# The opening of a two-layer transformer kernel, in quarters of the contraction

## The chip, the cores and the metric
The kernel runs on one core of a Trainium2 chip, as one program. The metric is the device time of one execution in microseconds (us). Engines: TensorE (PE, matmul; PEld its weight loads), VectorE (DVE), ScalarE (ACT), GpSimd (POOL), SyncE (SP, here only the issuer of DMAs). Each runs its own instruction list in order and waits on semaphores.

## The reference
Three layers on 256 tokens of width 1024, float32: one with sparse (top-k) attention and a gated convolution, one with pooling and latent attention, one with three attention branches. The change touches the start of the first:

```python
def first_block(x, c, ada_w, ada_b, ...):
    cond = jax.nn.silu(c)
    for l in range(DEPTH):
        mod = (cond @ ada_w[l] + ada_b[l])[:, None, :]
        sh_m, sc_m, g_m, sh_f, sc_f, g_f = jnp.split(mod, 6, axis=-1)
        h = x * (1.0 + sc_m) + sh_m
        if l % 2 == 0:
            e = l // 2
            y = even_mixer(h, ev_w_in[e], ev_conv_w[e], ev_w_out[e])
        ...
        x = layer_norm(DN_ALPHA * x + (1.0 + g_m) * y, ln_mix_g[l], ln_mix_b[l])
        ...
def even_mixer(h, w_in, conv_w, w_out):
    z = h @ w_in
    q, k, v, qi, ki, wi, bg, cg, xb = _split(z, EVEN_SIZES)
    ya = dsa_attention(q..., k..., v..., qi..., ki, wi)
    yb = bg * causal_dwconv(cg * xb, conv_w)
    return jnp.concatenate([ya, yb], axis=-1) @ w_out
```

In `dsa_attention` the index queries `qi`, index keys `ki` and weights `wi` give a score for each pair of tokens, of which the 64 highest are kept for each query; then softmax attention with 8 heads over q, k, v.

## The kernel before
**Units and precision.** Weights are cut into units of 256 columns (UC), 8 contraction blocks (kt) of 128 rows each, 1 MB. SP loads unit g into `raw[g % 2]` (`load_unit`), ScalarE rounds it into a high part `unit_hi` (`hi_unit`, L839), GpSimd subtracts to get the low part `unit_lo` (`lo_unit`, L727). The activations h are split likewise (`hh`, `hl`, from the whole `hf`). A product is high x high, high x low and low x high, summed in bank 4 + g % 2. Order of units: two of index queries (`G_QI`, g = 0, 1), `G_KI` (g = 2, index keys and weights, 192 columns), six of q, k, v (`G_QKV[DSA]`, g = 3 to 8; QKV 0 to 5 below), the convolution, the output.

**Waits in the loop of units.** SP loads unit g once the low part of unit g - 2 is made (`lo_up`). ScalarE converts unit g once unit g - 2 has filled its bank, for `unit_hi[g % 2]` is then free. TensorE starts on the high part and waits for the low one behind the first block of 128 columns.

**Modulation.** `cond @ ada_w` for the first layer's shift and scale (blocks 0, 1 and 2, 3 of 512 columns) is needed before h exists. Shift: VectorE sums `ada_w` row blocks times cond into 128 partial rows (`modulation_half`: half a is 4 contraction blocks x 512 columns, 1 MB), TensorE sums the partitions in one-column matmuls (`mod_columns`). Scale: TensorE multiplies directly (`mod_half`, cond as a one-column weight), ScalarE copies the row, and one-row matmuls turn it into columns. All 16 columns stand, then h is made for all of the contraction by VectorE and ScalarE (`h_columns`, `h_high`). The other halves (numbers 4 and up) are summed by VectorE between other work; their loads stand in SP's list beside those of certain units (`early`).

**Around it.** The small vectors are staged by POOL's DMAs and transposed on TensorE (`stage`), x is transposed in 16 steps (`transpose_rows`). After KI and QKV 0 come the index scores: heads 0 to 3, QKV 1, heads 4 to 7 (L1663). ScalarE applies relu, VectorE weights and adds them head by head (L2284, L2286), which frees the banks that the next heads write; ahead of that VectorE's list has the halves 4 to 7. Then VectorE takes the top 64, while TensorE does QKV 2 to 5.

Of the kernel before, what the change touches and what calls it, by code (L numbers as in the profile page):

```python
# [18 lines left out]
ALU = mybir.AluOpType  # L19
# [89 lines left out]
def build(nc, W, consts, out):  # L109
# [101 lines left out]
    turn(("modc", 0, 0), 6)  # L211
# [9 lines left out]
    ht_turns(0)  # L221
    for h in range(HEADS):
        turn(("idx", h), h % 4)
# [42 lines left out]
    with ctx:  # L266
# [123 lines left out]
        def down_home(d):  # L390

            if d in SPARE:
# [11 lines left out]
        mod_in = [sem(f"mod_in{i}") for i in range(2)]  # L404
# [27 lines left out]
                   FOX: (o_h[1], o_l[1]), MOBA: (o_h[2], o_l[2]), "stick": (o_h[0], o_l[0])}  # L432

# [154 lines left out]
        def _(sp_):  # L588
# [23 lines left out]
            def load_mod(e):  # L612

                if e >= 2:
                    sp_.wait_ge(mod_done, e - 1)
                s = e % 2
                sp_.dma_start(ada[2 + s].rearrange("p (t n) -> p t n", t=KD // 2), half_of(0, MOD_PE[e // 2], s)
                              ).then_inc(mod_in[s], 16)
# [209 lines left out]
        def _(act):  # L828
# [19 lines left out]
            def h_high(n, columns, scale, shift):  # L848

                evacuated(act, columns)  # L850
                if n == 0:

                    def whole(q):
                        o = full(act, ("ht", n, q))
                        for kt in (2 * q, 2 * q + 1):
                            ins = nc.scalar.activation(hf[:, kt, :], o[:, S * (kt % 2):S * (kt % 2 + 1)], ACT.Identity,
                                                       scale=scale[:, kt:kt + 1], bias=shift[:, kt:kt + 1])
                        ins.then_inc(free(("ht", n, q)), 1)

                    def high(q):  # L860
                        evacuated(act, ("ht", n, q))
                        k = slice(2 * q, 2 * q + 2)
                        nc.scalar.activation(hh[:, k, :], hf[:, k, :], ACT.Copy).then_inc(h_hi, 1)

                    whole(1)
                    high(0)
                    high(1)
                    whole(3)
                    high(2)
                    high(3)  # L870
                    return
# [155 lines left out]
            for i, j in enumerate(MOD_PE):  # L1027
                if i == 1:
                    hi_unit(0)
                act.wait_ge(mod_done, 2 * i + 2)  # L1030
                nc.scalar.activation(accg[0:1, AC * j:AC * (j + 1)], bank[4 + i][0:1, :], ACT.Copy).then_inc(mod_row, 1)
            h_high(0, ("modc", 0, 0), modT[:, 0, 8:16], modT[:, 0, 0:8])
            hi_unit(1)

# [222 lines left out]
        def _(pe):  # L1257
# [197 lines left out]
            def mod_columns(layer, parts, first=True, js=range(16)):  # L1455
# [3 lines left out]
                for i, part in enumerate(parts):  # L1459
                    for j in js:  # L1460
                        block = 6 * part + j // 4
                        k = P
                        if (layer, part) == (0, 0) and block in MOD_PE:
                            k = 1
                            pe.wait_ge(mod_row, MOD_PE.index(block) + 1)
                        elif j % 4 == 0:
                            summed(pe, layer, block)
# [3 lines left out]
                if j == 15:  # L1471
                    done(mm, name)

            def mod_half(e):

                i, s = e // 2, e % 2
                pe.wait_ge(mod_in[s], 16 * (i + 1))
# [1035 lines left out]
```

## Time and profile before

| | us |
|---|---|
| median of 3 runs (1187.02 to 1191.23) | 1189.29 |
| the profiled execution | 1187.67 |
| its span | 1185.9 |
| PE busy | 1127.9 (95%) |
| DVE busy | 538.6 (45%) |
| ACT busy | 590.7 (50%) |
| POOL busy | 831.8 (70%) |

The span is measured by the profiler from the first instruction to the last; the execution's own time has 1.8 us around it. Busy times overlap. Idle time of an engine is of interest where another one waits for it.

### The profile page before, as it was taken

To read this page: it belongs to the slowest core of one execution; us is meant where nothing else is said; L and a number is where in the kernel's file an instruction comes from. 1 tells how busy PE (TensorE), PEld (TensorE's weight loads), DVE (VectorE), ACT (ScalarE), POOL (GpSimd) and SP (SyncE) were. 2 spreads that over 40 slices of the span, in tenths; PEclk is the share of its full clock that TensorE was granted. 3 is DMA by queue.
4 is the path that set the end of the run, shared out by engine and by line. 5 is a ranking of instruction groups with operands and counts; after the bars stand their busy time and mean duration, and the time that the engine had idled before them with its cause. 6 is when DMAs were issued, how large, how long until landed. Compare 5 with 4: busy or idle time off the path is not lost.

```text
span 1185.9 us, 21675 instructions
## 1 busy us (share of the span) xinstructions
PE 1127.9 (95%) x8119; PEld 1033.5 (87%) x8119; DVE 538.6 (45%) x1120; ACT 590.7 (50%) x894; POOL 831.8 (70%) x297
## 2 busy tenths in 40 slices
PE   6899898999999988999999989999999999999997
PEld 2799788999998987989999969999999988999996
DVE  4668677965657684594323350433111333111112
ACT  0445425545453554545545434555776544455444
POOL 3567467988876634798788737566656776988885
PEclk9899998999999999999999999999999999999999
DMA  9987587999987354597666415434444544766652
GB/s 341 323 270 199 201 276 242 342 330 320 320 276 248 114 143 147 176 288 240 183 188 181 138 36 177 139 112 142 143 143 143 185 153 127 211 186 187 192 178 88
DMA packets 253485, 238.03 MB, mean 201 GB/s; under 512 B 18076, under 2 KB 216529, under 8 KB 253425
## 3 DMA queue, kind: packets, MB, share of 16 engines
q1 hardware_dynamic: 235104, 198.70, 54.4%
q10 hardware_dynamic: 17712, 38.28, 9.0%
q8 instruction: 41, 0.67, 0.2%
q0 software_dynamic: 608, 0.22, 0.1%
q14 instruction: 20, 0.16, 0.0%
HBM read 236.12 MB, written 1.05 MB: 200 GB/s over the span
## 4 chain that ended last, share of the span: by engine, by line
PE 68%; DMA 7%; ACT 7%; DVE 7%; POOL 6%; issue 3%; SPq 0%; ACTq 0%; DVEq 0%; POOLq 0%
PE bank L1270 16%; PE bank L1271 16%; PE bank L1272 16%; POOL unit_lo L727 5%; ACT unit_hi L839 3%; DMA raw<-in_ev_w_in 3%; PE bank L1304 2%; PE bank L1295 2%; DMA raw<-in_ffn_w_up 2%; PE bank L1408 2%; PE bank L1296 2%; DMA ada<-in_ada_w 2%; PE bank L1331 1%; DVE x L2029 1%; PE bank L1324 1%
## 5 line engine op out<-in xcount | busy, mean ns | idle before, releaser
L727 POOL TENSOR_TENSOR unit_lo<-raw,unit_hi 128x2048 fp32r<-128x2048 f32 (+4 forms) x88 | 348.1, 3960 | 231.5 <-ACT unit_hi L839 230.6
L1270 PE MATMUL bank<-h_hi,unit_hi 128*128 128x256 f32 x1152 | 327.8, 285 | 2.9 <-POOL unit_lo L779 2.9
L1271 PE MATMUL bank<-h_lo,unit_hi 128*128 128x256 f32 x1152 | 326.6, 284 | 0.0
L1272 PE MATMUL bank<-h_hi,unit_lo 128*128 128x256 f32 x1152 | 326.6, 283 | 0.0
L779 POOL TENSOR_TENSOR unit_lo<-raw,unit_hi 128x2048 fp32r<-128x2048 f32 (+1 forms) x70 | 257.2, 3674 | 70.1 <-ACT unit_hi L986 65.2
L1270 PEld LDWEIGHTS bank<-h_hi,unit_hi 128*128 128x128 f32 x1152 | 221.5, 192 | 8.3 <-issue 5.5
L1271 PEld LDWEIGHTS bank<-h_lo,unit_hi 128*128 128x128 f32 x1152 | 221.5, 192 | 2.5
L1272 PEld LDWEIGHTS bank<-h_hi,unit_lo 128*128 128x128 f32 x1152 | 221.4, 192 | 0.0
L839 ACT ACTIVATE unit_hi<-raw 128x2048 fp32r<-128x2048 f32 (+4 forms) x98 | 163.1, 1666 | 103.4 <-DMA raw<-in_ffn_w_up 28.6
L782 POOL TENSOR_TENSOR down<-raw_down,down 128x1024 fp32r<-128x1024 f32 x70 | 176.5, 2522 | 0.0
L2160 DVE SCALAR_TENSOR_TENSOR work<-bank,cols,work 128x254 f32<-128x254 f32 (+1 forms) x176 | 72.6, 474 | 130.2 <-ACT work L973 130.2
L1270 PE MATMUL bank<-down,y_hi 128*128 128x512 f32 x296 | 116.5, 394 | 1.8 <-issue 0.9
L1271 PE MATMUL bank<-down,y_hi 128*128 128x512 f32 x296 | 116.0, 392 | 0.0
L1272 PE MATMUL bank<-down,y_lo 128*128 128x512 f32 x296 | 115.2, 389 | 0.0
L986 ACT ACTIVATE unit_hi<-raw 128x2048 fp32r<-128x2048 f32 (+1 forms) x60 | 90.8, 1514 | 5.1 <-DMA raw<-in_ffn_w_up 4.2
L971 ACT ACTIVATE work<-bank,cols 128x256 f32<-128x256 f32 x44 | 20.9, 474 | 118.2 <-PE bank L1272 105.2
L2189 DVE TENSOR_TENSOR bank<-bank,work 128x256 f32<-128x256 f32 x32 | 13.8, 433 | 135.3 <-ACT work L976 135.3
L1295 PE MATMUL bank<-h_hi,unit_hi 128*128 128x256 f32 x272 | 70.0, 294 | 2.5 <-DVE h_full L2313 2.5
L1012 ACT ACTIVATE down<-raw_down 128x1024 fp32r<-128x1024 f32 x60 | 63.3, 1056 | 14.5 <-PE bank L1272 14.4
L1296 PE MATMUL bank<-h_lo,unit_hi 128*128 128x256 f32 x272 | 68.5, 288 | 0.0
L1270 PEld LDWEIGHTS bank<-down,y_hi 128*128 128x128 f32 x296 | 55.8, 189 | 12.3 <-issue 1.9
L1272 PEld LDWEIGHTS bank<-down,y_lo 128*128 128x128 f32 x296 | 55.6, 188 | 12.1
(361 smaller groups left out, 2180.3 us busy)
## 6 DMA issues: line engine op xcount, KB each, us to landing
raw<-in_ffn_w_up SPq DMA_DIRECT2D x88, 512.0 KB, 5.2
raw<-in_w_in SPq DMA_DIRECT2D x60, 512.0 KB, 4.5
raw_down<-in_ffn_w_down SPq DMA_DIRECT2D x44, 512.0 KB, 5.5
ada<-in_ada_w ACTq DMA_DIRECT2D x16, 1024.0 KB, 6.9
raw<-in_w_up SPq DMA_DIRECT2D x64, 256.0 KB, 3.0
raw_down<-in_w_down SPq DMA_DIRECT2D x32, 512.0 KB, 3.5
raw<-in_ev_w_in SPq DMA_DIRECT2D x28, 512.0 KB, 5.2
att<-in_ada_w ACTq DMA_DIRECT2D x14, 1024.0 KB, 7.3
```

What stands on the lines that cost most here:

```text
L727: nc.gpsimd.tensor_tensor(ul[g % 2][:, w], raw[g % 2][:, w], uh[g % 2][:, w].bitcast(F32), ALU.subtract).then_inc(lo_up, 1)
L779: nc.gpsimd.tensor_tensor(ul[s][:, 0:w], raw[s][:, 0:w], uh[s][:, 0:w].bitcast(F32), ALU.subtract).then_inc(lo_up, 1)
L782: nc.gpsimd.tensor_tensor(down[:, 1 - k, 1, :], rawd[1 - k][:, :], down[:, 1 - k, 0, :].bitcast(F32), ALU.subtract).then_inc(lo_dn, 1)
L839: nc.scalar.activation(uh[s][:, w], raw[s][:, w], ACT.Copy).then_inc(hi_up, 1)
L986: nc.scalar.activation(uh[s][:, 0:w], raw[s][:, 0:w], ACT.Copy).then_inc(hi_up, 1)
L1012: nc.scalar.activation(down[:, 1 - k, 0, :], rawd[1 - k][:, :], ACT.Copy).then_inc(hi_dn, 1)
L1270: nc.tensor.matmul(o, sh, mh, start=first, stop=False)
L1271: nc.tensor.matmul(o, sh, ml, start=False, stop=False)
L1272: return nc.tensor.matmul(o, sl, mh, start=False, stop=last)
L1295: nc.tensor.matmul(o[:, 0:S], uh[s][:, a], mh[:, kt, :], start=kt == 0, stop=False)
L1296: nc.tensor.matmul(o[:, 0:S], uh[s][:, a], ml[:, kt, :], start=False, stop=False)
L2160: return V.scalar_tensor_tensor(t[:, back:S], bank[4 + s][:, S * j:S * (j + 1) - back], w, t[:, back:S], ALU.mult, ALU.add)
```

## The change
The shift and scale of the first layer are made in four quarters of 256 columns, which are two contraction blocks (kt) of h each. For a quarter, SP loads 2 MB in four DMAs (`load_first`), VectorE sums the shift in 8 steps of 256 columns (`first_sum`), TensorE multiplies the scale (`first_product`), four small matmuls give the columns (`first_columns`), VectorE makes two blocks of h and the low part (`first_rows`), ScalarE the high part. Between the quarters TensorE does the index-query products of both units for the contraction blocks that exist: high parts (`first_highs`), h's low parts (`first_rests`), and one quarter later the unit's low parts (`first_lows`). x and the two units are loaded behind quarter 0. The loads of halves 4 and up move: halves 4 and 5 from ahead of KI to behind KI and QKV 0, and 6 to 10 one or two units later.

```diff
-            for a in range(MOD_START):
-                load_ada(a)
-                load_mod(a)
-                if a == MOD_START - 2:
-                    sp_.dma_start(x[:, :, :], W["x"][0].rearrange("(t p) n -> p t n", p=P)).then_inc(x_in, 16)
+            load_first(0)
+            sp_.dma_start(x[:, :, :], W["x"][0].rearrange("(t p) n -> p t n", p=P)).then_inc(x_in, 16)
             for g in range(2):
                 load_unit(g)
-            for a in SUM_FIRST:
-                load_ada(a)
-            early = {G_KI: SUM_EARLY[0], G_QKV[DSA][0]: SUM_EARLY[1], G_QKV[DSA][2]: SUM_IDX, G_QKV[DSA][3]: SUM_ATT[0],
-                     G_QKV[DSA][4]: SUM_ATT[1]}
+            for q in range(1, 4):
+                load_first(q)
+            early = {G_KI: SUM_FIRST[0], G_QKV[DSA][0]: SUM_FIRST[1], G_QKV[DSA][1]: SUM_EARLY[0], G_QKV[DSA][2]: SUM_EARLY[1], G_QKV[DSA][3]: SUM_IDX,
+                     G_QKV[DSA][4]: SUM_ATT[0], G_QKV[DSA][5]: SUM_ATT[1]}
...
+            def load_first(q):
+
+                s = q % 2
+                if q >= 2:
+                    sp_.wait_ge(ada_acc, q - 1)
+                    sp_.wait_ge(mod_done, q - 1)
+                for piece in range(2):
+                    for home, c, landed in ((ada[s], UC * q, first_in), (ada[2 + s], D + UC * q, mod_in)):
...
-            h_high(0, ("modc", 0, 0), modT[:, 0, 8:16], modT[:, 0, 0:8])
-            hi_unit(1)
+            for q in range(4):
+                act.wait_ge(mod_done, q + 1)
+                c = slice(D + UC * q, D + UC * (q + 1))
+                nc.scalar.activation(accg[0:1, c], first_row(q), ACT.Copy).then_inc(mod_row, 1)
+                evacuated(act, ("ht", 0, q))
+                k = slice(2 * q, 2 * q + 2)
+                nc.scalar.activation(hh[:, k, :], hf[:, k, :], ACT.Copy).then_inc(h_hi, 1)
+                for g in range(2) if q == 0 else ():
+                    hi_unit(g)
...
-            mod_columns(0, (0,), js=[0, 1, 2, 3, 8, 9, 10, 11])
-            mod_half(3)
-            mod_columns(0, (0,), first=False, js=[4, 5, 6, 7, 12, 13, 14, 15])
-            first_units(0, G_QI[:1], low_last=True)
-            unit_cols(G_QI[1], hh, hl)
+            first_columns(0)
+            first_highs(0)
+            for g in G_QI:
+                first_rests(0, g)
+            evacuated(pe, "stage")
+            for q in range(1, 4):
+                first_product(q)
+                for g in G_QI:
+                    first_lows(q - 1, g)
+                first_columns(q)
+                first_highs(q)
+                for g in G_QI:
+                    if q == 3:
+                        first_lows(q, g)
+                    mm = first_rests(q, g, q == 3)
...
+            def first_sum(q):
+
+                s, acc = q % 2, bank[7][:, 0:UC]
+                for kt in range(KD):
...
+                    if kt == 0:
+                        link(V.tensor_scalar(dst, w, cond[:, 0:1], None, ALU.mult))
+                    elif kt < KD - 1:
+                        link(V.scalar_tensor_tensor(dst, w, cond[:, kt:kt + 1], acc, ALU.mult, ALU.add))
+                    else:
+                        V.scalar_tensor_tensor(dst, w, cond[:, kt:kt + 1], acc, ALU.mult, ALU.add).then_inc(ada_acc, 1)
+
+            def first_rows(q):
+
+                o = full(dve, ("first", q))
+                sh, sc = (modT[:, 0, 8 * i + 2 * q:8 * i + 2 * q + 2] for i in range(2))
+                link(V.scalar_tensor_tensor(sc, o[:, 2:4], 1.0, sc, ALU.add, ALU.add))
+                V.tensor_tensor(sh, o[:, 0:2], sh, ALU.add).then_inc(free(("first", q)), 1)
...
+                for i in range(2):
+                    kt = 2 * q + i
+                    ins = V.tensor_scalar(hf[:, kt, :], o[:, S * i:S * (i + 1)], modT[:, 0, 8 + kt:9 + kt],
+                                          modT[:, 0, kt:kt + 1], ALU.mult, ALU.add)
...
+                dve.wait_ge(h_hi, q + 1)
+                k = slice(2 * q, 2 * q + 2)
+                V.tensor_tensor(hl[:, k, :], hf[:, k, :], hh[:, k, :].bitcast(F32), ALU.subtract).then_inc(h_lo_dve, 1)
+
+            first_sum(0)
...
+            first_rows(0)
+            for q in range(1, 4):
+                first_sum(q)
+                first_rows(q)
```

TensorE's list before, from the last modulation product to the first products of the index-query unit 0 (bank6 takes the columns, unit_hi0 is that unit's high part):

```order
L1469 MATMUL bank6<-consts,accg 128x1 [waits ada_acc,bank_free6]
L1469 MATMUL bank6<-consts,accg 128x1 x3
L1469 MATMUL bank6<-consts,accg 128x1 [waits mod_row] x4
L1480 MATMUL bank5<-accg,cols 1x512 [waits mod_in1]
L1480 MATMUL bank5<-accg,cols 1x512 x3
L1469 MATMUL bank6<-consts,accg 128x1 [waits ada_acc]
L1469 MATMUL bank6<-consts,accg 128x1 x3
L1469 MATMUL bank6<-consts,accg 128x1 [waits mod_row] x4
L1408 MATMUL bank4<-h_hi,unit_hi0 128x256 [waits h_hi,hi_up]
```

The same list now, from the product of quarter 1 to the high products behind its columns (bank4 and bank5 take the two units):

```order
L1467 MATMUL bank6<-accg,cols 1x256 [waits mod_in01,mod_row,bank_free6]
L1467 MATMUL bank6<-accg,cols 1x256 x3
L1467 MATMUL bank6<-accg,cols 1x256 [waits mod_in11]
L1467 MATMUL bank6<-accg,cols 1x256 x3
L1490 MATMUL bank4<-h_hi,unit_lo0 128x256 [waits lo_up]
L1490 MATMUL bank4<-h_hi,unit_lo0 128x256 x3
L1490 MATMUL bank5<-h_hi,unit_lo1 128x256 [waits lo_up]
L1490 MATMUL bank5<-h_hi,unit_lo1 128x256 x3
L1477 MATMUL bank0<-consts,accg 128x1 [waits ada_acc,bank_free0]
L1477 MATMUL bank0<-consts,accg 128x1
L1481 MATMUL bank0<-consts,accg 128x1 [waits mod_row]
L1490 MATMUL bank4<-h_hi,unit_hi0 128x256 [waits h_hi]
```

Where no dense product stood ahead of the columns, the low products of both units for the quarter before now stand ahead of those of quarters 1 to 3.

SP's list before, from the halves 4 and 5 to the load of QKV 2 (raw0 by 192 columns is KI; raw1 behind it QKV 0; att and ada1 are the two homes of the modulation halves):

```order
L624 DMA att<-in_ada_w 128x4x512 [waits ada_acc]
L624 DMA ada1<-in_ada_w 128x4x512 [waits ada_acc]
L610 DMA raw0<-in_ev_w_in 128x4x192 [waits lo_up]
L610 DMA raw0<-in_ev_w_in 128x4x192
L624 DMA att<-in_ada_w 128x4x512 [waits ada_acc]
L610 DMA raw1<-in_ev_w_in 128x4x256 [waits lo_up]
L610 DMA raw1<-in_ev_w_in 128x4x256
L624 DMA ada1<-in_ada_w 128x4x512 [waits ada_acc]
L610 DMA raw0<-in_ev_w_in 128x4x256 [waits lo_up]
L610 DMA raw0<-in_ev_w_in 128x4x256
L646 DMA consts<-shape_constants 128x1600
L610 DMA raw1<-in_ev_w_in 128x4x256 [waits lo_up]
```

And now, from the load of KI on:

```order
L617 DMA raw0<-in_ev_w_in 128x4x192
L635 DMA att<-in_ada_w 128x4x512 [waits ada_acc]
L617 DMA raw1<-in_ev_w_in 128x4x256 [waits lo_up]
L617 DMA raw1<-in_ev_w_in 128x4x256
L635 DMA ada1<-in_ada_w 128x4x512 [waits ada_acc]
L617 DMA raw0<-in_ev_w_in 128x4x256 [waits lo_up]
L617 DMA raw0<-in_ev_w_in 128x4x256
L635 DMA att<-in_ada_w 128x4x512 [waits ada_acc]
L654 DMA consts<-shape_constants 128x1600
L617 DMA raw1<-in_ev_w_in 128x4x256 [waits lo_up]
L617 DMA raw1<-in_ev_w_in 128x4x256
L635 DMA ada1<-in_ada_w 128x4x512 [waits ada_acc]
```

Half 6 (the att row ahead of the constants) stood behind KI and now stands behind QKV 1; half 7 (the last ada1 row) stood behind QKV 0 and now behind QKV 2.

## Rows read from the trace of the kernel before

**Rows 1.** Stretches: length, busy (instructions) of PE, PEld, DVE, ACT, POOL, PEclk, DMA share, GB/s.

```profile
36.00:38.30 2.30, 0.05 (x2) 0.04 (x1) 2.14 (x6) 1.80 (x4) 2.30 (x1) 0.50 1.05 386
...
46.30:52.00 5.70, 5.70 (x50) 5.70 (x50) 3.68 (x5) 1.97 (x2) 4.32 (x2) 1.00 1.03 362
52.00:57.80 5.80, 5.80 (x51) 5.80 (x50) 2.67 (x5) 2.51 (x2) 2.96 (x1) 1.00 1.08 375
```

**Rows 2.** Waits of PE, 36 to 230 us: total, times, longest us.

```profile
PE bank L1295 <- DVE h_full L2313: 2.5, 1, 2.5
...
PE bank L1537 <- DVE y_lo L2083: 1.8, 1, 1.8
```

**Rows 3.** Timeline from 0 us (start, us, instruction); then DMA issues: KB, landing us.

```profile
9.27 1.91 POOL L793 DMA_DIRECT2D work<-in_ada_b  x4
...
10.15 6.26 PE L1480 MATMUL bank<-att,cols 128*1 128x512 f32 x8 [6.51 <-DMA att<-in_ada_w]
...
16.24 3.60 PE L1480 MATMUL bank<-accg,cols 128*1 128x512 f32 x8
...
raw<-in_ev_w_in SPq DMA_DIRECT2D x24, 512.0 KB, 5.2
...
work<-in_ada_b POOLq DMA_DIRECT2D x4, 8.0 KB, 4.9
```

**Rows 4.** Timeline, 25 to 46 us: the chain up to the first unit.

```profile
25.54 1.91 PE L1451 MATMUL bank<-consts,x 128*128 128x128 f32 x16
...
27.34 2.34 DVE L1903 SCALAR_TENSOR_TENSOR bank<-ada,cols,bank 128x512 f32<-128x512 f32 x3
...
32.56 1.91 ACT L839 ACTIVATE unit_hi<-raw 128x2048 fp32r<-128x2048 f32 x1 [12.10 <-DMA raw<-in_ev_w_in]
...
34.56 4.51 POOL L727 TENSOR_TENSOR unit_lo<-raw,unit_hi 128x2048 fp32r<-128x2048 f32 x1 [23.38 <-ACT unit_hi L839]
...
36.09 0.17 DVE L1925 SCALAR_TENSOR_TENSOR cols<-bank,cols 128x8 f32<-128x8 f32 x1 [5.62 <-PE bank L1469]
...
36.49 1.90 DVE L1959 TENSOR_SCALAR h_full<-bank,cols 128x256 f32<-128x256 f32 x4
37.52 1.15 ACT L863 ACTIVATE h_hi<-h_full 128x512 fp32r<-128x512 f32 x2
...
38.30 3.93 PE L1408 MATMUL bank<-h_hi,unit_hi 128*128 128x256 f32 x16 [2.25 <-ACT h_hi L863]
38.31 3.19 DVE L1982 TENSOR_TENSOR h_lo<-h_full,h_hi 128x512 fp32r<-128x512 f32 x4
...
44.31 2.08 PE L1408 MATMUL bank<-h_hi,unit_lo 128*128 128x256 f32 x16
```

**Rows 5.** Timeline, 46 to 52 us: evacuation, conversion and low part of KI.

```profile
46.43 0.60 ACT L888 ACTIVATE h_full<-bank 128x512 f32<-128x512 f32 x1 [4.00 <-PE bank L1408]
...
46.92 1.48 ACT L839 ACTIVATE unit_hi<-raw 128x1536 fp32r<-128x1536 f32 x1
...
48.48 3.51 POOL L727 TENSOR_TENSOR unit_lo<-raw,unit_hi 128x1536 fp32r<-128x1536 f32 x1 [1.36 <-ACT unit_hi L839]
```

**Rows 6.** Timeline: half 7's end, the index weighting, the second index scores.

```profile
58.19 0.75 DVE L1903 SCALAR_TENSOR_TENSOR accg<-ada,cols,bank 128x512 f32<-128x512 f32 x1
67.53 0.74 DVE L2284 TENSOR_SCALAR work<-bank,small 128x128 f32<-128x128 f32 x2 [8.59 <-ACT bank L1047]
68.37 2.43 DVE L2286 SCALAR_TENSOR_TENSOR work<-bank,small,work 128x128 f32<-128x128 f32 x6
...
71.27 1.58 PE L1663 MATMUL bank<-att,h_full 64*128 64x128 f32 x16
```

**Rows 7.** Timeline of DVE at 109 us: two steps over 255 columns.

```profile
109.55 1.00 DVE L2313 SCALAR_TENSOR_TENSOR h_full<-bank,cols,h_full 128x255 f32<-128x255 f32 x2
```

**Rows 8.** PE: 16 transposes at 181 us; a stretch behind the wait that ends at 137.4.

```profile
180.75 3.65 PE L1451 MATMUL bank<-consts,x 128*128 128x128 f32 x16 [4.67 <-DVE x L2014]
...
138.40:140.40 2.00, 2.00 (x12) 0.51 1.05 371
```

More of the change, by code:

```diff
@@ L221, in build @@
     ht_turns(0)
+    turn(("first", 0), 7)
+    for q in range(1, 4):
+        turn(("first", q), q - 1)
     for h in range(HEADS):
@@ L403, in build @@
         ada_in = [sem(f"ada_in{i}") for i in range(2)]
-        mod_in = [sem(f"mod_in{i}") for i in range(2)]
+        first_in = [[sem(f"first_in{i}{j}") for j in range(2)] for i in range(2)]
+        mod_in = [[sem(f"mod_in{i}{j}") for j in range(2)] for i in range(2)]
         hi_up, lo_up, hi_dn, lo_dn = sem("hi_up"), sem("lo_up"), sem("hi_dn"), sem("lo_dn")
@@ L850, in h_high @@
                 evacuated(act, columns)
[L851 to L871, printed above, removed]
                 for q in range(4):
@@ L1461, in mod_columns @@
                         block = 6 * part + j // 4
[L1462 to L1466, printed above, removed]
+                        if j % 4 == 0:
                             summed(pe, layer, block)
                         c = block_at(layer, block).start + P * (j % 4)
-                        mm = nc.tensor.matmul(o[:, 16 * i + j:16 * i + j + 1], accg[0:k, c:c + P], ones[0:k, 0:1],
+                        mm = nc.tensor.matmul(o[:, 16 * i + j:16 * i + j + 1], accg[:, c:c + P], ones[:, 0:1],
                                               start=True, stop=True)
@@ L1481, in mod_half, with first_columns @@
                                           start=kt == 0, stop=kt == KD - 1)
                 mm.then_inc(mod_done, 1)
+            def first_columns(q):
+                o = begin(("first", q))
+                pe.wait_ge(ada_acc, q + 1)
+                for j in range(2):
+                    c = UC * q + P * j
+                    nc.tensor.matmul(o[:, j:j + 1], accg[:, c:c + P], ones[:, 0:1], start=True, stop=True)
+                pe.wait_ge(mod_row, q + 1)
+                for j in range(2):
+                    c = D + UC * q + P * j
+                    mm = nc.tensor.matmul(o[:, 2 + j:3 + j], accg[0:1, c:c + P], ones[0:1, 0:1], start=True, stop=True)
+                done(mm, ("first", q))
@@ new lines, in first_part @@
+            def first_part(g, q, weight, h, last=False):
+                o, s = bank[4 + g % 2], g % 2
+                for kt in (2 * q, 2 * q + 1):
+                    for i in range(2):
+                        a = slice(slot(g) + kt * UC + P * i, slot(g) + kt * UC + P * i + P)
+                        mm = nc.tensor.matmul(o[:, S * i:S * (i + 1)], weight[s][:, a], h[:, kt, :],
+                                              start=kt == 0 and i == 0 and weight is uh and h is hh,
+                                              stop=last and kt == KD - 1 and i == 1)
+                return mm
@@ L1484, in late_rows, with first_highs, first_lows, first_rests @@
+            def first_highs(q):
+                pe.wait_ge(h_hi, q + 1)
+                for g in G_QI:
+                    if q == 0:
+                        unit_begin(g)
+                    first_part(g, q, uh, hh)
+            def first_lows(q, g):
+                pe.wait_ge(lo_up, g + 1)
+                first_part(g, q, ul, hh)
+            def first_rests(q, g, last=False):
+                pe.wait_ge(h_lo_dve, q + 1)
+                return first_part(g, q, uh, hl, last)
             def late_rows(f):
@@ L1630, in _ @@
             evacuated(pe, "cond")
-            for half in range(3):
-                mod_half(half)
+            first_product(0)
             pe.wait_ge(stage_in, 16 * len(STAGED))
@@ L1973, in h_columns @@
                     return
-                for q in (0, 2) if n == 0 else (1, 0, 3, 2):
-                    if n and q % 2 == 0:
+                for q in (1, 0, 3, 2):
+                    if q % 2 == 0:
                         dve.wait_ge(h_hi, highs(n, 2 * q + 1))
                     whole(q)
-                for q in range(4) if n == 0 else (3,):
+                for q in (3,):
                     evacuated(dve, ("ht", n, q))
@@ L2268, in _ @@
             evacuated(dve, "stage")
-            modulation_half(MOD_START - 1, bank[7][:, :])
-            mod_columns(0, (0,))
-            h_columns(0, modT[:, 0, 8:16], modT[:, 0, 0:8])
+            first_rows(0)
+            for q in range(1, 4):
+                first_sum(q)
+                first_rows(q)
             for a in SUM_FIRST + SUM_EARLY:
```

50 lines of the change are left out of this document (28 added, 22 removed).

## The prediction

> **What bounds the kernel now.** I read the table of stretches first [rows 1]. From 46.3 us on TensorE is busy without a gap and a unit of 256 weight columns takes 5.7 to 5.8 us, so a microsecond that reaches the start of this stretch reaches the end. Before 38.3 us almost nothing of the dense work runs, while the DMA engines are full (share above 1). The opening is therefore bound by bytes (8 MB of modulation weights, 1 MB of x, 2 MB for two units) and by the short chain behind them: columns, h, high part, first product. The wait list of TensorE over 36 to 230 us [rows 2] holds seven entries; behind this opening, up to 160 us, the largest are 2.5 and 1.8 us: little slack behind the opening that could swallow a delay.
>
> The timeline of the start [rows 3] gives the clock and the late small loads; that around 25 to 43 us [rows 4] the price of each link; 46 to 52 us [rows 5] what the third unit (KI) needs after a bank is full; 58 to 71 us [rows 6] that VectorE waits 8.59 us for the first index scores because its modulation halves were done at 58.9. [Rows 7, 8] price a 256 column sum and TensorE at the low clock.
>
> **The change, part by part.** I work in the profile's own times and follow the two gates that TensorE's program now has: the quarters, then the second group of index scores, which before starts at 71.27 [rows 6] and is followed by dense work.
>
> *Bytes.* The same 11 MB must land. At 362 GB/s [rows 1] 1 MB takes 2.9 us; a unit's loads take 5.2 us from issue [rows 3], that is about 2.3 us plus 2.9. New order: quarter 0 (2 MB) near 10 us, x 13, the two index-query units 19, quarter 1 near 25, quarter 2 near 31.
>
> *Quarter 0.* TensorE transposes the staged rows first. Their last load is issued by POOL at about 10.7 (9.27 plus 1.91 less one issue) and lands 4.9 us later [rows 3], so 15.7. Before, this was hidden: the transposes stood behind three modulation products. Then 16 transposes of x. [...] With the little work ahead of it now I take half speed: 4 + 16 transposes at the 3.65 us per 16 of [rows 8] end at 20.5 (at full clock 1.91, [rows 4]). Columns (4 small matmuls) 0.6, VectorE 0.17 + 0.17 and two h blocks at 0.48, with hand-overs 1.5, ScalarE high part 0.6 to 0.7 [rows 4]: high part at 23.4. Only now, in ScalarE's program, come the two conversions of the units, 1.91 each, until 27.2; they had data since 19. POOL follows with 4.51 twice [rows 4] and hand-overs: low parts at 30 and 34.7.
>
> *Quarter 1.* TensorE's program has the low products of BOTH units for quarter 0 ahead of the columns of quarter 1. They wait for the second low part, 34.7. So columns(1) are done at 35.8 though their sum is ready at about 27. VectorE and ScalarE as above: high part(1) at 38.1. The old kernel had all of h by 40.6.
>
> *Quarters 2 and 3.* Two bounds of a period. VectorE: low part of h 0.8, sum of 8 steps, columns 0.6, h 1.5, high part 0.7. The trace has no 256-column sum; the nearest row is L2313 with 255 columns, 1.00 for two, 0.52 from start to start with the hand-over [rows 7]; 8 of them are 4.2. Period 7.8. (If a step cost half of the 512-column one, 2.34 us for 3 in [rows 4], the sum would be 3.1 and the period 6.7; this is the lower end. The row shows 0.50 for half the width against 0.756, so I take it.) TensorE: 8 + 8 products, 2.1 at full clock or 3.9 at half (16 took 2.08 and 3.93, [rows 4]), a modulation product of 8 x 256 columns at half of 3.60 or of 6.26 [rows 3], 8 low products at half of 2.08 or 3.93, columns 0.6, then 2.2 us of idling for VectorE and ScalarE: 7.7 at full clock, 11.8 at half. The granted clock is 0.50 in the wait for h at 36 to 38.3 [rows 1], behind a stretch of one-column matmuls, and 0.51 behind the 2.5 us wait that ends at 137.4 [rows 2, 8]. Every quarter now has such a gap. I take 9.0, between. High part(3): 38.1 + 18 = 56.1.
>
> The Trainium skill, "VectorE: DVE Perf Modes", section "The TRN2 errata", says that an instruction on SBUF data pays a fixed cost, and advises tiles of 512 elements or more. By that rule 32 steps of 256 cost more than 16 of 512, and the trace agrees by its own numbers above: 2 x 0.50 against 0.756.
>
> *Tail and the third unit.* Behind high part(3): 8 + 4 + 4 products until the first unit is full, 1.9 to 3.8, taken 2.8: 58.9. Then as in [rows 5]: evacuation and conversion of KI, 46.43 to 48.40 and a hand-over, 2.1 together, so the conversion ends at H = 61.0; POOL's low part 3.5: 64.5. Before, this conversion and low part lay under the second index-query unit; now both units fill together and nothing covers them. KI: first block 16 products, wait for 64.5, 8 + 24 products 3.9, end 68.4 (before 57.8). QKV 0 ends 74.2, first index scores (1.58) 75.8, QKV 1 81.6.
>
> *The second gate.* SP's list now puts modulation halves 6 and 7 behind the loads of QKV 1 and QKV 2 (before one and two units earlier), and those wait for the low parts of KI (64.5) and QKV 0 (69). From 64.5 the DMA engines must deliver in order QKV 1, half 6, 0.8 MB of constants, QKV 2, half 7: 4.8 MB x 2.9 + 2.3 = 16.2, so 80.7. VectorE sums half 7 in 3.1: 83.8. Only then the index weighting of heads 0 and 1, 0.82 each [rows 6], frees two banks for the second group of scores: 85.5, and heads 2 and 3 for the last of them: TensorE leaves the scores at 87.9, waiting about 4.5 us for banks. What queues behind the waiting scores is QKV 2 and all later units; ScalarE's evacuations wait with them. Before, that moment was 71.27 + 1.58 = 72.85. Difference +15. Upper path without this wait: 81.6 + 1.6 = 83.2, +10.3.
>
> *Later.* VectorE's top-k starts about as much later as TensorE does, so it gives nothing back. Raw loads get a few microseconds more ahead of TensorE during its wait; of the stalls in [rows 2] I let 1.5 us go. Sum +13.5, and the profiled execution's 1187.67 (span 1185.9) becomes 1201.2. It lies 1.6 below the median of the runs shown, 1189.29; I forecast the median and put it between the two bases: 1202.
>
> Costed at nothing: the removed ScalarE h blocks (2.0 us, not on the new path before the conversions), smaller row copies (under 0.3 us each, beside VectorE's sum), two more semaphores.
>
> **Rivals.**
> - *Faster: quarters overlap as drawn.* Sums and products keep up with the DMA, quarter 3 lands near 36, its columns at 39, high part at 41, both units full at 44.5. Then KI is converted at 46.5 and the second scores end 22.2 after it without a bank wait: 68.7, -4. It turns positive once H passes 50.6. For it: bytes alone allow it. Against it: the program order behind POOL's second low part, and 7.8 us a quarter on VectorE even at full clock. With the bank wait it would be 46.5 + 26.9 = 73.4, no change. 1184 to 1190.
> - *Only the first gate.* Halves 6 and 7 land soon enough for the banks. +9 to +11: 1198 to 1200, or 1196 with the quick period of 7.8 (H = 58.6).
> - *TensorE stays at half clock through the quarters.* Period 11 to 11.8: H = 66 to 67.5, with the bank wait +20 to +21.5, less 1.5: 1208 to 1210.
> - *Absorbed.* The late kernel's other waits give back nearly all: within 3 us. Against it: [rows 1], dense from 46.3.
>
> **How the numbers follow.** Forecast (both gates, clock mixed) 0.50, its own range 1198 to 1206; first gate only 0.24; half clock throughout 0.15; faster rival 0.05; absorbed or cancelled 0.06. 0.3% is 3.6 us, about what a measurement of this kernel tells from no change. Slower takes the first three, 0.89; same 0.06; faster 0.05. Range 1194 to 1209: the lower end is the first gate with short periods and a full-clock start (transposes 1.9 instead of 3.65), the upper end the lower half of the slow clock case; what is left out is the faster rival, the absorbed case and the rest of the slow one.
>
> **What would show it.** Right: POOL's second low part ends near 35 and columns(1) directly behind it; periods of 8 to 11 us between high parts; a granted clock of 0.5 in parts of 36 to 60; the KI conversion ends near 61 and TensorE idles around it; halves 6 and 7 reach VectorE after 75; the second scores wait for banks. Wrong: KI's conversion before 51, or VectorE still idle ahead of the index weighting, or stretches behind 90 us that run shorter than before by more than 3 us.

## The result, and the profile after

| | before | after |
|---|---|---|
| median, us (range, runs) | 1189.97 (1187.02 to 1193.26, 6) | 1210.23 (1207.84 to 1215.05, 6) |
| profiled execution, span | 1187.67, 1185.9 | 1209.55, 1207.4 |
| conversion of KI ends (H) | 48.40 | 63.46 |
| second index scores end | 72.85 | 92.32 |
| evacuation of QKV 2 starts (ScalarE) | 78.84 | 99.67 |
| first power of the even mixer (POOL) | 176.78 | 197.49 |

The ratio is 1.0175 [1.0158, 1.0192]: slower by 20.3 us. The forecast was 1202 in a range of 1194 to 1209: the sign held and both gates are there, the size is off. Nearly all of the loss is there by 100 us (20.8); behind it the two traces run in parallel to within 1 us (20.7 at the first power, 21.5 at the end of the span).

TensorE of the changed kernel; the rows answer to [rows 3, 4]. Columns as there: start, us, instruction, count, in brackets the idle time ahead and what ended it.

```profile
16.01 1.91 PE L1440 MATMUL bank<-consts,x 128*128 128x128 f32 x16
...
27.48 5.11 PE L1467 MATMUL bank<-accg,cols 128*1 128x256 f32 x16
32.52 1.21 PE L1490 MATMUL bank<-h_hi,unit_lo 128*128 128x256 f32 x8
...
36.74 1.59 PE L1490 MATMUL bank<-h_hi,unit_hi 128*128 128x256 f32 x8 [2.14 <-ACT h_hi L1020]
38.13 1.91 PE L1490 MATMUL bank<-h_lo,unit_hi 128*128 128x256 f32 x8
39.97 4.00 PE L1467 MATMUL bank<-att,cols 128*1 128x256 f32 x16
43.90 1.22 PE L1490 MATMUL bank<-h_hi,unit_lo 128*128 128x256 f32 x8
44.96 0.50 PE L1477 MATMUL bank<-consts,accg 128*128 128x1 f32 x4
45.39 0.60 PE L1481 MATMUL bank<-consts,accg 1*128 1x1 f32 x4
48.13 2.08 PE L1490 MATMUL bank<-h_hi,unit_hi 128*128 128x256 f32 x8 [2.14 <-ACT h_hi L1020]
...
51.50 3.61 PE L1467 MATMUL bank<-accg,cols 128*1 128x256 f32 x16
...
88.98 3.34 PE L1701 MATMUL bank<-att,h_full 64*128 64x128 f32 x16 [4.39 <-DVE work L2357]
```

A period can be added up from it, 36.74 to 48.13: high and low-h products 3.23, the scale product of the next quarter 3.93, low products 1.06, columns 1.03, and 2.14 idle. The scale product, L1467, is the largest item. Its rows say x16: eight matmuls, two instructions each. The column matmuls show the same (two at L1477 and two at L1481, x4 and x4). The products of the rounded parts (tiles of type fp32r, x8 for eight) and the transposes (x16 for 16) stand once.

VectorE of the changed kernel: for [rows 4] the columns of quarters 1 to 3, for [rows 7] the sum of quarter 2, for [rows 6] the end of half 7.

```profile
34.63 0.16 DVE L2314 SCALAR_TENSOR_TENSOR cols<-bank,cols 128x2 f32<-128x2 f32 x1 [7.51 <-PE bank L1481]
...
37.91 3.12 DVE L2306 SCALAR_TENSOR_TENSOR bank<-att,cols,bank 128x256 f32<-128x256 f32 x6
41.06 0.48 DVE L2308 SCALAR_TENSOR_TENSOR accg<-att,cols,bank 128x256 f32<-128x256 f32 x1
46.03 0.16 DVE L2314 SCALAR_TENSOR_TENSOR cols<-bank,cols 128x2 f32<-128x2 f32 x1 [4.49 <-PE bank L1481]
...
57.18 0.16 DVE L2314 SCALAR_TENSOR_TENSOR cols<-bank,cols 128x2 f32<-128x2 f32 x1 [4.24 <-PE bank L1481]
...
84.21 2.34 DVE L1941 SCALAR_TENSOR_TENSOR bank<-ada,cols,bank 128x512 f32<-128x512 f32 x3 [5.70 <-DMA ada<-in_ada_w]
...
87.25 0.74 DVE L2355 TENSOR_SCALAR work<-bank,small 128x128 f32<-128x128 f32 x2
```

The sum is ready at 41.54 and its columns are read at 46.03: in quarters 1 to 3 VectorE waits 7.51, 4.49 and 4.24 us for TensorE. So TensorE's row of work, not VectorE's, sets the period. Later, before the index weighting (L2355), VectorE has its last idle stretch on a load of half 7, where before it was idle for want of scores [rows 6].

ScalarE and, below it, POOL of the changed kernel; [rows 4, 5] are the ones before.

```profile
20.33 0.63 ACT L1020 ACTIVATE h_hi<-h_full 128x512 fp32r<-128x512 f32 x1 [5.42 <-DVE h_full L2320]
20.86 3.70 ACT L847 ACTIVATE unit_hi<-raw 128x2048 fp32r<-128x2048 f32 x2
...
36.05 0.63 ACT L1020 ACTIVATE h_hi<-h_full 128x512 fp32r<-128x512 f32 x1 [3.06 <-DVE h_full L2320]
...
47.45 0.63 ACT L1020 ACTIVATE h_hi<-h_full 128x512 fp32r<-128x512 f32 x1 [3.07 <-DVE h_full L2320]
...
58.60 0.63 ACT L1020 ACTIVATE h_hi<-h_full 128x512 fp32r<-128x512 f32 x1 [3.08 <-DVE h_full L2320]
...
61.98 1.48 ACT L847 ACTIVATE unit_hi<-raw 128x1536 fp32r<-128x1536 f32 x1
```

```profile
22.84 9.01 POOL L735 TENSOR_TENSOR unit_lo<-raw,unit_hi 128x2048 fp32r<-128x2048 f32 x2 [11.66 <-ACT unit_hi L847]
63.53 8.06 POOL L735 TENSOR_TENSOR unit_lo<-raw,unit_hi 128x1536 fp32r<-128x1536 f32 x2 [31.68 <-ACT unit_hi L847]
```

Four high parts, 11.40 and 11.15 us apart for the last two steps, and POOL without work from 31.85 to 63.53.

Stretches of the changed kernel, columns as in [rows 1]. The stretch that was dense at 362 GB/s now has TensorE idle for 1.8 of 5.7 us and the DMA engines half empty. 85 to 95 us are the wait for banks and what stands behind it; the granted clock is 0.86 over the first half and 0.50 over the second, where most of the second scores and the start of QKV 2 run.

```profile
46.30:52.00 5.70, 3.87 (x19) 3.47 (x20) 4.69 (x11) 0.63 (x1) 0.00 (x0) 0.70 0.53 172
...
85.00:90.00 5.00, 1.02 (x7) 0.96 (x8) 4.61 (x10) 2.13 (x2) 2.70 (x2) 0.86 0.94 307
90.00:95.00 5.00, 4.96 (x25) 3.71 (x22) 4.79 (x10) 1.72 (x4) 3.74 (x1) 0.50 0.93 323
```

### The profile page after: what moved, and what is told of

Same layout as the page of the kernel before. It is cut to its first block, busy times and chain, and to the rows that moved or that the text cites. A ratio compares the mean times of both kernels' runs of the same rounds, so it can differ in the third digit from the quotient of the medians.

```text
span 1207.4 us, 21783 instructions
## 1 busy us (share of the span) xinstructions
PE 1135.5 (94%) x8151; PEld 1039.6 (86%) x8151; DVE 544.9 (45%) x1146; ACT 588.9 (49%) x892; POOL 831.2 (69%) x297
## 3 DMA queue, kind: packets, MB, share of 16 engines
HBM read 236.12 MB, written 1.05 MB: 196 GB/s over the span
## 4 chain that ended last, share of the span: by engine, by line
PE 71%; POOL 8%; ACT 6%; DVE 6%; DMA 5%; issue 4%; SPq 0%; ACTq 0%; POOLq 0%; DVEq 0%
PE bank L1259 17%; PE bank L1260 17%; PE bank L1261 17%; POOL unit_lo L735 4%; ACT unit_hi L847 3%; PE bank L1293 2%; PE bank L1284 2%; PE bank L1285 2%; DMA raw<-in_ev_w_in 2%; DMA raw<-in_ffn_w_up 1%; PE bank L1490 1%; PE bank L1397 1%; PE bank L1320 1%; PE bank L1467 1%; PE bank L1313 1%
## 5 line engine op out<-in xcount | busy, mean ns | idle before, releaser
L1260 PE MATMUL bank<-h_lo,unit_hi 128*128 128x256 f32 x1144 | 324.3, 284 | 0.0
L958 ACT ACTIVATE work<-bank,cols 128x256 f32<-128x256 f32 x44 | 20.8, 474 | 116.6 <-PE bank L1261 104.3
L1285 PE MATMUL bank<-h_lo,unit_hi 128*128 128x256 f32 x264 | 66.8, 289 | 0.0
L1261 PEld LDWEIGHTS bank<-down,y_lo 128*128 128x128 f32 x296 | 55.6, 188 | 12.1
```

What stands on the lines that cost most here:

```text
L1260: nc.tensor.matmul(o, sh, ml, start=False, stop=False)
L1261: return nc.tensor.matmul(o, sl, mh, start=False, stop=last)
L1285: nc.tensor.matmul(o[:, 0:S], uh[s][:, a], ml[:, kt, :], start=False, stop=False)
```

## The experiments

The theory after the result was: two gates in series. The quarters delay H by 15.1 us, more than the 12.6 of the prediction because the scale product was priced at half of what it takes; then half 7 arrives too late and holds the banks for the second scores. Behind each figure stands the interval of the ratio to the kernel before, run beside it. "Faster than the change" sets medians of different rounds side by side; the medians of the kernel before differ by 0.8 us between these rounds, and the intervals reach 4 to 5 us to either side for e1 to e4, 2 to 3 for e5 to e8. Differences of 2 or 3 us in the whole are therefore not shown by the times alone.

Two experiments, e1 and e4, leave TensorE's list of the opening as it is in the changed kernel, and so show how much one opening varies from execution to execution:

| | scale products 1 to 3 | periods | H |
|---|---|---|---|
| changed kernel | 5.11, 4.00, 3.61 | 11.40, 11.15 | 63.46 |
| e1_loads | 4.24, 3.61, 3.61 | 11.24, 9.89 | 62.75 |
| e4_warm | 4.18, 3.61, 3.61 | 11.22, 9.89 | 63.07 |

H is known to 0.7 us, a single period is not. In e1 the last period ran at a granted clock near 1 (0.96 from 46 to 57 us) and the tail behind it at 0.50 (57 to 61.5 us), so the time from high part(3) to H was 5.84 us in place of 4.23.

**Halves 6 and 7 ahead of the load of QKV 1** (e1_loads)

```diff
-early = {G_KI: SUM_FIRST[0], QKV0: SUM_FIRST[1], QKV1: SUM_EARLY[0], QKV2: SUM_EARLY[1], QKV3: SUM_IDX, ...}
+early = {G_KI: SUM_FIRST[:1], QKV0: SUM_FIRST[1:] + SUM_EARLY, QKV2: [SUM_IDX], QKV3: SUM_ATT[:1], ...}
```

Halves 8 and up also go one unit earlier again.

> The changed kernel with one thing put back: modulation halves 6 and 7 are issued behind the load of QKV 0, ahead of that of QKV 1, and halves 8 to 10 one unit earlier again, as before. Theory A (the second gate is the late landing of half 7 and nothing else): half 7 is summed by 75 instead of 87.3 us, VectorE waits for the first relu again, TensorE no longer waits 4.4 us for banks at 84.6 and does not fall to the low clock there (3.34 us for the second index scores go back to about 1.6); second scores end near 86.2 instead of 92.3 and the whole is 7.5 to 9.5 us faster than the changed kernel, about 1201.5. Rival B (the wait would only be taken over by the raw load of QKV 2, whose conversion waited until 87.2): at most 3 us faster. Rival C (DMA order does not matter, VectorE's top-k decides): no change, 1210.

Measured 1205.13 (1204.30 to 1207.81), ratio 1.0142 [1.0107, 1.0177]. ScalarE, VectorE, then TensorE of this kernel:

```profile
46.39 0.63 ACT L1020 ACTIVATE h_hi<-h_full 128x512 fp32r<-128x512 f32 x1 [3.06 <-DVE h_full L2320]
...
56.28 0.63 ACT L1020 ACTIVATE h_hi<-h_full 128x512 fp32r<-128x512 f32 x1 [3.08 <-DVE h_full L2320]
```

```profile
72.41 0.75 DVE L1941 SCALAR_TENSOR_TENSOR accg<-ada,cols,bank 128x512 f32<-128x512 f32 x1
80.21 0.74 DVE L2355 TENSOR_SCALAR work<-bank,small 128x128 f32<-128x128 f32 x2 [7.06 <-ACT bank L1036]
```

```profile
83.82 1.58 PE L1701 MATMUL bank<-att,h_full 64*128 64x128 f32 x16
```

Half 7 is summed at 73.2, VectorE waits for scores again, and the second scores take 1.58 us without a wait and end at 85.4, 6.9 earlier. The first power comes 6.3 earlier, the whole is 5.1 faster. The second gate is real and worth about 6 us: the scores end 22.6 behind H in place of 28.9 (the no-wait path of the prediction said 22.2). The mechanism is theory A's; its size for the whole, 7.5 to 9.5, was too high.

**Half of the scale product** (e2_half_product)

```diff
+                    if q and kt % 2:
+                        continue
                     mm = nc.tensor.matmul(first_row(q), cond[:, kt:kt + 1], ...
-                                          start=kt == 0, stop=kt == KD - 1)
+                                          start=kt == 0, stop=kt == (KD - 2 if q else KD - 1))
```

> The changed kernel with half of the scale products of quarters 1 to 3 left out (4 of 8 contraction blocks; that part of the computation is missing). Theory A (the quarter's period is set by TensorE, and the scale product of 8 blocks by 256 columns takes 3.5 us at full clock and 5.1 at low, twice what the prediction took): periods between high parts of h fall from 11.4 and 11.15 to about 9.4, the conversion of KI ends near 58.0 instead of 63.5 (product 1 gives 2 to 2.5, products 2 and 3 1.8 each), the whole is 4.5 to 6.5 us faster than the changed kernel. Rival B (VectorE's sum of 4.2 us plus its chain sets the period, about 7.3 us, and TensorE's list only looks full): no change of the period. Rival C (fewer matmuls lower the clock for longer and eat the gain): less than 2 us.

Measured 1207.75 (1205.54 to 1209.30), ratio 1.0160 [1.0124, 1.0197]. TensorE of this kernel:

```profile
27.46 3.34 PE L1469 MATMUL bank<-accg,cols 128*1 128x256 f32 x8
30.73 0.73 PE L1492 MATMUL bank<-h_hi,unit_lo 128*128 128x256 f32 x4
31.92 0.74 PE L1492 MATMUL bank<-h_hi,unit_lo 128*128 128x256 f32 x4 [0.45 <-POOL unit_lo L735]
...
39.39 2.51 PE L1469 MATMUL bank<-att,cols 128*1 128x256 f32 x8
...
48.61 3.01 PE L1469 MATMUL bank<-accg,cols 128*1 128x256 f32 x8
```

The periods are 10.4 and 9.7, H is 59.96 (2.8 to 3.5 below the three openings of the table above), and the first power comes 5.1 earlier. The whole is 2.5 faster, which the times alone do not show. The direction is A's, at less than its size, and the rows show why. Four matmuls for eight saved 1.77, 1.49 and 0.60 us against the changed kernel, 0.90, 1.10 and 0.60 against e1, never half of the product: TensorE was granted less (36 to 48 us: 0.78, where the changed kernel, e4 and e1 have 0.84, 0.86 and 0.88). That is rival C in part; that the missing matmuls lowered the clock fits the rows and is not shown by them. And in quarter 1 the wait that the prediction had named, on POOL's second low part, now appears, at 0.45 us: it was right behind the product all along.

**The product of the next quarter moved into TensorE's wait** (e3_product_ahead)

```diff
+            first_product(1)
             for q in range(1, 4):
-                first_product(q)
                 for g in G_QI:
                     first_lows(q - 1, g)
                 first_columns(q)
+                if q < 3:
+                    first_product(q + 1)
                 first_highs(q)
```

> The changed kernel with the scale product of quarter q+1 moved from behind the index-query products of quarter q to between the columns of q and them, so that it runs while VectorE and ScalarE make h; nothing is left out. Theory A: it fills the 2.1 us in which TensorE waits for h in quarters 1 and 2, but product 2 and 3 outlast that gap by 1.5 us or more; periods fall by 2.1 us each to about 9.2, and the clock stays at 1.00 there; the conversion of KI ends near 59 instead of 63.5, the whole 3.5 to 5 us faster. Rival B (the product has to wait for its DMA there, since quarter 3 is issued only behind product 1): periods stay above 10.5, under 1.5 us faster. Rival C (VectorE sets the period): unchanged.

Measured 1205.24 (1204.18 to 1206.63), ratio 1.0137 [1.0103, 1.0171]. TensorE of this kernel:

```profile
33.55 3.62 PE L1467 MATMUL bank<-att,cols 128*1 128x256 f32 x16
37.09 1.21 PE L1490 MATMUL bank<-h_hi,unit_hi 128*128 128x256 f32 x8
...
40.71 0.58 PE L1477 MATMUL bank<-consts,accg 128*128 128x1 f32 x4 [0.49 <-DVE accg L2310]
...
48.91 0.58 PE L1477 MATMUL bank<-consts,accg 128*128 128x1 f32 x4 [0.48 <-DVE accg L2310]
...
83.17 3.34 PE L1703 MATMUL bank<-att,h_full 64*128 64x128 f32 x16 [4.08 <-DVE work L2359]
```

The same work in another order: the wait for the high part is filled, the granted clock is 1.00 from 36 to 48 us, and the period is 8.20, a microsecond below what was expected and now set by VectorE's sum (TensorE waits 0.49 for it). The tail pays a part back: from 48 to 60 us the clock is 0.72, and H follows high part(3) by 5.84 us. H is 57.95, 5.5 earlier, the first power 4.6 earlier, the whole 5.0 faster. The bank wait of 4.08 us stays, as half 7 is still late.

**TensorE kept busy ahead of the second scores** (e4_warm)

```diff
+                if p == 2:
+                    evacuated(pe, "wi")
+                    for _ in range(4):
+                        nc.tensor.matmul(bank[6][:, :], ident, x[:, 0, 0:512], start=True, stop=True)
```

> The changed kernel with four dummy matmuls (x by the identity, 512 columns, float32, 0.86 us each at full clock) ahead of the second index scores, where TensorE waits 4.4 us for banks. Theory A: the wait itself stays, but the second scores run at full clock (1.6 to 1.9 us instead of 3.34) and QKV 2 behind them too, so TensorE gets 2 to 3.5 us back and the whole is 1.5 to 3.5 us faster. Rival B (the low clock there cost nothing, since the scores wait for VectorE to free banks one after the other at 0.82 us a head): under 0.7 us.

Measured 1213.99 (1209.45 to 1216.85), ratio 1.0201 [1.0158, 1.0244]. TensorE of this kernel:

```profile
84.06 3.60 PE L1700 MATMUL bank<-x,consts 128*128 128x512 f32 x8
88.48 0.93 PE L1705 MATMUL bank<-att,h_full 64*128 64x128 f32 x8 [0.82 <-DVE work L2361]
90.17 1.41 PE L1705 MATMUL bank<-att,h_full 64*128 64x128 f32 x8 [0.77 <-DVE work L2361]
```

The scores end at 91.6, 28.5 behind H in place of 28.9: the clock cost at most 0.4 us there, and the pairs start 1.69 apart, each behind a wait for a bank that VectorE frees. Theory A fell at the scores, B held: the 3.34 us are pacing by VectorE. The first power comes 1.4 earlier than in the changed kernel: 0.4 of it are there at H already, 0.3 come at the scores, 0.7 behind them. So the whole's 3.8 above the changed kernel does not come from the opening. In the profiled execution 3.1 us of it arise between two later powers (last section); the rest stays open, and the times of the two kernels overlap (1209.45 to 1216.85 and 1207.84 to 1215.05). The first row settles something else: four float32 matmuls of 512 columns are x8 and 3.60 us, the row that [rows 3] shows at L1480.

**e1 and e3 together** (e5_both; the diff is the sum of both)

> The changed kernel with both repairs: modulation halves 6 and 7 issued ahead of the load of QKV 1, and the scale product of quarter q+1 between the columns of quarter q and its index-query products. Theory A (two gates in series: the gains add): KI's conversion ends near 58 as with the product ahead alone, the second scores 22.5 us behind it near 80.5 instead of 92.3; against the changed kernel 9 to 12 us faster, about 1199.5. Rival (the second gate hides behind the first, or another load takes its place): no faster than the better of the two alone, 1203 or more.

Measured 1199.44 (1197.60 to 1200.80), ratio 1.0080 [1.0063, 1.0097]: 10.8 faster than the change, against 5.1 and 5.0 alone. H 58.24, second scores end 80.9, first power 12.1 earlier. The gains add, as theory A said: the two gates stand one behind the other.

**Only the first index-query unit between the quarters** (e6_one_unit, on e5)

```diff
-                for g in G_QI:
+                for g in G_QI[:1]:
                     ...
+            unit_cols(G_QI[1], hh, hl)
             unit_cols(G_KI, hh, hl, blocks=(64, 0))
```

The other loops over G_QI in the opening are cut to the first unit in the same way.

> As the kernel with both repairs, but only the first index-query unit is multiplied between the quarters; the second is done whole behind it, as before the change. Theory A (with two units between the quarters nothing is left to cover conversion and low part of KI, 2.1 + 3.6 us): KI's products follow the second unit without a wait, start near 57.5 and end 5.1 us later near 62.5, against about 67.6 with both units between the quarters; QKV 0 and all later units 3 to 5 us earlier, the whole 3 to 5 us faster than with both units between, about 1195. Rival B (the dense work moved behind high part 3 costs as much as the cover gives): within 1.5 us of the kernel with both units between the quarters.

Measured 1198.34 (1195.17 to 1202.38), ratio 1.0081 [1.0052, 1.0110]: the interval covers that of e5. TensorE of this kernel:

```profile
38.80 0.58 PE L1477 MATMUL bank<-consts,accg 128*128 128x1 f32 x4 [1.93 <-DVE accg L2311]
```

KI is converted at 55.19, 3.0 earlier and under dense work, but the second scores end at 80.8, where e5 has 80.9. The period stays 8.20, as VectorE sets it, and TensorE now waits 1.93 us for the sum in place of 0.49. Rival B holds: a cover made of work that had filled gaps costs what it covers.

**The kernel before with its halves loaded as late as in the change** (e7_before_late)

```diff
-            early = {G_KI: SUM_EARLY[0], QKV0: SUM_EARLY[1], QKV2: SUM_IDX, QKV3: SUM_ATT[0], QKV4: SUM_ATT[1]}
+            early = {QKV1: SUM_EARLY[0], QKV2: SUM_EARLY[1], QKV3: SUM_IDX, QKV4: SUM_ATT[0], QKV5: SUM_ATT[1]}
```

> The kernel before with one thing of the change alone: SP issues modulation halves 6 and 7 behind the loads of QKV 1 and QKV 2 (and 8 to 10 one unit later). Theory A (those loads are short of time even in the old opening): half 7 lands near 68 instead of 55.8, its sum ends near 72 instead of 58.9, the index weighting starts 4.5 us later, the second index scores wait for banks and end near 76 to 77 instead of 72.85; the whole 3 to 4.5 us slower than before. Rival (only the late quarters make these loads late): within 1 us of before.

Measured 1194.63 (1194.18 to 1195.62), ratio 1.0043 [1.0027, 1.0060], +5.5 us. TensorE of this kernel, where [rows 6] has 1.58 us at 71.27:

```profile
74.77 3.35 PE L1663 MATMUL bank<-att,h_full 64*128 64x128 f32 x16 [2.50 <-DVE work L2286]
```

The second gate alone, without any quarter, costs 5.5 us in the whole. In the profiled execution the scores end 5.3 later and the first power comes 4.8 later, but 0.9 of that are there at H (49.32 for 48.40), ahead of which this run has one load less and none more: the gate itself is 4.4 at the scores, 28.8 behind H for 24.4. Half 7 is there at 70.0 (68 expected). Theory A holds, at a size at or a little above the upper end of its range.

**The quarters with every wait filled that could be** (e8_tuned, on e5)

```diff
             first_columns(0)
+            first_product(1)
+            first_columns(1)
             first_highs(0)
             ...
-            for q in range(1, 4):
+            for q in range(1, 3):
+                first_product(q + 1)
                 first_highs(q)
                 ...            # products of h_lo, then the low products of q - 1
+                first_columns(q + 1)
```

Also hi_unit(0) stands ahead of the first high part on ScalarE, and POOL makes the low parts of h in place of VectorE.

> As the kernel with both repairs, and further: the conversion of index-query unit 0 ahead of the first high part, the low parts of h on POOL instead of VectorE, product and columns of quarter 1 ahead of the index-query products of quarter 0, low products behind all others. Theory A (a quarter costs VectorE 4.2 us of sum and 2.2 us of columns and h, TensorE 7.2 us, so 3 periods of about 7.2 behind columns(1) at 29 are the floor): high part 3 ends near 46 to 47, KI's conversion near 51; against before within 3 us, 1187 to 1192. Rival B (the DMA sets the floor: quarter 3 lands near 37, high part 3 near 41): 4 us or more faster than before. Rival C (the low clock in the gaps): high part 3 near 50, 3 to 6 us slower than before.

Measured 1193.71 (1190.26 to 1194.16, 5 runs), ratio 1.0029 [1.0013, 1.0046]. ScalarE, then TensorE of this kernel:

```profile
31.87 0.63 ACT L1027 ACTIVATE h_hi<-h_full 128x512 fp32r<-128x512 f32 x1 [2.12 <-DVE h_full L2332]
...
41.46 0.63 ACT L1027 ACTIVATE h_hi<-h_full 128x512 fp32r<-128x512 f32 x1 [4.99 <-DVE h_full L2332]
...
48.94 0.63 ACT L1027 ACTIVATE h_hi<-h_full 128x512 fp32r<-128x512 f32 x1 [4.98 <-DVE h_full L2332]
...
52.31 1.48 ACT L852 ACTIVATE unit_hi<-raw 128x1536 fp32r<-128x1536 f32 x1
```

```profile
23.50 5.85 PE L1474 MATMUL bank<-accg,cols 128*1 128x256 f32 x16 [4.72 <-DMA accg<-in_ada_w]
...
74.86 1.58 PE L1713 MATMUL bank<-att,h_full 64*128 64x128 f32 x16
```

A stretch of it, columns as in [rows 1]:

```profile
36.00:48.00 12.00, 12.00 (x86) 9.66 (x86) 5.66 (x16) 1.38 (x3) 1.26 (x1) 1.00 0.91 289
```

It is 16.5 faster than the change and still slower than before: by 4.6 us from median to median, by 3.4 from the ratio. Its second scores end at 76.4, 3.6 behind 72.85. High part(3) ends at 49.57 and KI's conversion at 53.79, where theory A said 46 to 47 and 51: these are the figures of rival C (near 50, 3 to 6 slower). Its cause, the low clock, holds for one piece only: the product of quarter 1 took 5.85 us for 3.61, at a granted clock of 0.50 from 23.5 to 26 us. From 36 to 60 us the clock is 1.00. There TensorE has no idle time up to 48 us, and its own list makes the two steps between high parts: 7.48 us for the last, near theory A's 7.2, and 9.59 for the one before, which also holds 2.1 us of index-query products of quarter 0. Full DMA engines (rival B) don't set it: they move 289 GB/s from 36 to 48 us and 248 from 48 to 60. No version beat the kernel before, which had the high part of all of h at 40.6.

## Why the prediction was wrong in size

*The failed step* is the size of one term of the sum for quarters 2 and 3, "a modulation product of 8 x 256 columns at half of 3.60 or of 6.26". The row of [rows 3] reads 128x512 x8, and I took it for eight matmuls of 512 columns. It is one half: four matmuls (the loop at L1480 runs over four blocks), each two instructions in the trace. A quarter's eight matmuls of 256 columns have as many columns, and measured 5.11, 4.00 and 3.61 against the 1.8 to 3.1 in the sum. With the right price the bounds of the period were 9.5 and 14.9, and 9.0, which lay a third of the way between 7.7 and 11.8, becomes 11.2. The two measured periods, 11.40 and 11.15, are together 4.6 us longer than the predicted 18. That the count is two instructions for one matmul is shown by e4; that the product stands on the path of the period is shown by e3 (same product moved into the wait, period 8.20) and, less clearly, by e2.

The product is not the whole of the 4.6 us. At the same third of the way it had been given 2.2 us and took 3.93 and 3.54, 1.7 and 1.3 more. The columns, four small matmuls, had 0.6 and took 1.03, which is the same miscount: eight instructions had taken 1.05 in the kernel before. The rest, 0.6 and 0.7, is in the high and low-h products, 3.23 and 3.37 for 2.7, that is in the clock. How much the clock takes differs from execution to execution: with product and columns at their full-clock price the sum for a period is 9.9, which the last period of e1 and e4 shows (9.89). That the corrected third of the way gives 11.2 is partly luck.

Point by point:
- *Quarter 0.* High part at 20.96, predicted 23.4: an error of 2.4 in the other direction. Half speed for the transposes was an assumption. No run shows the 16 transposes of x at 3.65 us in the opening; they took 1.91 in this one and in every other trace, here behind a product of 6.36 us and 1.08 us of idling.
- *Quarter 1.* The program order did hold columns(1) until 34.60 (35.8 predicted), but the last to end there was the product (32.6), with POOL's low part at 31.85 just ahead. High part(1) ends at 36.68, for 38.1, which takes 1.4 us off the error of the periods.
- *VectorE's period.* The sum of eight steps took 4.14, for 4.2, and where VectorE set the period (e3, e5) it was 8.2, for 7.8; the 0.4 are the columns. It was not what bound the changed kernel. The Trainium skill ("VectorE: DVE Perf Modes", section "The TRN2 errata") gives instructions that read SBUF a fixed cost each. This trace agrees: 0.48 us for 256 columns, which is more than half of the 0.75 for 512.
- *Tail and KI.* High part(3) ends at 59.23 for 56.1, H is 63.46 for 61.0; the way between them took 4.23 for 4.9. As said, nothing covers KI's conversion: TensorE waits 1.10 and 1.39 us.
- *The second gate.* Half 7 landed at 84.2 for 80.7 and the scores ended 28.9 behind H, for 26.9. Of these 2.0 us, 1.0 is the landing, counted from H, and 0.9 the scores: they had 2.4 from the first free bank (85.5 to 87.9) and took 3.34, paced by VectorE (e4). The wait itself was forecast at about 4.5 and is 4.39. The mechanism is shown from both sides, by e1 and e7.
- *Given back.* 1.5 us were to go from later stalls; none did. The stalls of 2.5 and 1.8 are 2.5 and 2.3 in the changed kernel, and 1.4 us more are lost behind the second scores, where the clock is 0.50: evacuation of QKV 2 follows their end by 7.35 us, before by 5.99. Of these, 1.2 are left at the first power.

In sum: 4.4 at the end of the second scores (2.5 at H and 2.0 behind it), 2.7 by the first power (1.5 not given back, 1.2 more) and 0.8 in the rest make, before rounding, the 8.0 us by which the span's 21.5 exceeds the predicted 13.5. Right were the two gates themselves and the order in which they follow. The first came to 15.1 us for 12.6, the second (scores behind H, less the path without a wait) to 6.2 for 4.7. The rival "half clock throughout" came closest in time (1208 to 1210), for a wrong reason: the clock was mixed (0.77, 0.84 and 0.87 in the stretches from 26 to 60 us).

## What to carry to other kernels

Before a row's duration is scaled, count the instructions in the code and compare the count with the trace's: a float32 matmul stands there twice. When a phase is cut into pieces that go round several engines, price the whole turn, once per piece, and place work that needs nothing from the turn inside its wait: here that order alone was worth 5 us of the 20. Before one profile of an opening is read to a tenth, look at how far a second execution of the same list lies from it. And when units move earlier, look at which loads were moved behind them; the late halves cost the kernel before 5.5 us by themselves (e7).

## What was not expected of the hardware

- A float32 matmul shows as two instructions, 0.45 us each at 512 columns at full clock (x8, 3.60 for four), while an fp32r matmul shows as one (x16 for 16 of 256 columns, 2.08 us at full clock, [rows 4]).
- Removed work can be worth less than its price. Half of the scale product taken away saved 0.60 to 1.77 us, where the whole product took 3.61 to 5.11, at a granted clock of 0.78 in place of 0.84 to 0.88 from 36 to 48 us. The same work moved into a wait (e3) went with a clock of 1.00 in that stretch, and 0.72 in the next.
- The granted clock of the same list differs from execution to execution: the scale product of quarter 1 took 5.11, 4.24 and 4.18 us in three of them.
- What the opening wins arrives only roughly at the end. A stretch of the later program, between two powers on POOL, takes 76.6 us in some profiled executions (408.02 to 484.58 before, 429.57 to 506.22 after, also e1 and e3) and 78.0 to 79.7 in the others (426.39 to 505.79 in e2, 431.98 to 511.69 in e4); the first power was the cleaner measure of an opening.
